# First stage of a two-block transformer kernel: x loaded first, squares summed on TensorE and VectorE, half of the modulation made as rows

## What is computed

```python
silu_c = jax.nn.silu(c)
silu_cc = jax.nn.silu(c_ctx)[None]
mod = jnp.split((silu_c @ ada_w[l] + ada_b[l])[:, None, :], N_MOD, axis=-1)
mod_c = jnp.split((silu_cc @ ada_w[l] + ada_b[l])[:, None, :], N_MOD, axis=-1)

def rmsnorm(x, g):
    xf = x.astype(jnp.float32)
    xf = xf * lax.rsqrt(jnp.mean(xf * xf, axis=-1, keepdims=True) + EPS)
    return (xf * g.astype(jnp.float32)).astype(x.dtype)

def modulate(h, shift, scale):
    return h * (1.0 + scale) + shift

t_ctx = mixer_inputs(modulate(rmsnorm(xc, norm_mix_g[l]), mod_c[0], mod_c[1]), w_in[l], ...)
t_lat = mixer_inputs(modulate(rmsnorm(x, norm_mix_g[l]), mod[0], mod[1]), w_in[l], ...)
```

## Time and profile before

| | us |
|---|---|
| median of 3 runs | 5051.04 |
| lowest and highest run | 5043.8 and 5053.86 |
| profiled execution | 5049.76 |
| its span, first to last instruction | 5047.7 |
| TensorE busy in it | 4843.0 (96%) |
| VectorE busy | 3071.4 (61%) |
| ScalarE busy | 1904.8 (38%) |
| GpSimd busy | 1260.1 (25%) |

### The profile page before, as it was taken

How to read it: one execution, slowest core, us unless ns; L and a number is a source line. 1 busy time by engine, 2 the same in 40 slices (tenths; PEclk the granted TensorE clock), 3 DMA queues, 4 the chain that set the end, 5 groups by cost and what they waited for, 6 DMA issues and landing times.

```text
span 5047.7 us, 66502 instructions
## 1 busy us (share of the span) xinstructions
PE 4843.0 (96%) x27141; PEld 4084.6 (81%) x27141; DVE 3071.4 (61%) x5232; ACT 1904.8 (38%) x2848; POOL 1260.1 (25%) x1007
## 2 busy tenths in 40 slices
PE   7999999999899999999999999999999899999999
PEld 6888878788779998987678787888888677767787
DVE  4545455689768898996543526366667444454555
ACT  3445322235833333333442426232223443353332
POOL 1111000036755666762220013100000210020000
PEclk8999999999999999999999999999999999999999
DMA  4111124423568998984101010222332121112222
GB/s 164 51 47 68 43 84 142 167 86 109 208 246 316 343 352 335 354 317 164 51 26 60 30 61 22 88 79 105 118 117 86 42 68 38 59 34 102 92 92 75
DMA packets 157310, 636.24 MB, mean 126 GB/s; under 512 B 12384, under 2 KB 62704, under 8 KB 106448
## 3 DMA queue, kind: packets, MB, share of 16 engines
q1 hardware_dynamic: 112688, 467.97, 25.5%
q0 software_dynamic: 42240, 160.88, 8.5%
q10 hardware_dynamic: 2080, 3.15, 0.2%
HBM read 595.25 MB, written 36.70 MB: 125 GB/s over the span
## 4 chain that ended last, share of the span: by engine, by line
PE 84%; DVE 7%; ACT 4%; POOL 2%; DMA 2%; issue 2%; SPq 0%; DVEq 0%; ACTq 0%; POOLq 0%
PE banks L280 70%; PE banks L3128 4%; PE banks L3247 2%; PE banks L3220 2%; DVE oa L2374 1%; PE banks L1020 1%; DMA X<-ctxT_in 1%; PE banks L396 1%; PE banks L358 1%; ACT high L214 1%; PE banks L952 1%; DVE nt L525 1%; PE banks L1011 1%; DVE cols L3152 1%; DVE low L229 1%
## 5 line engine op out<-in xcount | busy, mean ns | idle before, releaser
L229 DVE TENSOR_TENSOR low<-raw,high 128x2048 fp32r<-128x2048 f32 (+3 forms) x335 | 740.4, 2211 | 653.1 <-ACT high L214 653.0
L280 PE MATMUL banks<-UH,high 128*128 128x512 f32 (+2 forms) x2816 | 1041.7, 370 | 44.6 <-DVE UL L515 13.4
L280 PE MATMUL banks<-UH,low 128*128 128x512 f32 (+2 forms) x2816 | 1015.8, 361 | 0.0
L280 PE MATMUL banks<-UL,high 128*128 128x512 f32 (+2 forms) x2816 | 1015.4, 361 | 0.0
L214 ACT ACTIVATE high<-raw 128x2048 fp32r<-128x2048 f32 (+3 forms) x341 | 619.5, 1818 | 670.1 <-PE banks L280 332.4
L280 PEld LDWEIGHTS banks<-UH,high 128*128 128x128 f32 (+1 forms) x2816 | 533.1, 189 | 152.7 <-issue 51.8
L280 PEld LDWEIGHTS banks<-UH,low 128*128 128x128 f32 (+1 forms) x2816 | 533.5, 189 | 87.2
L280 PEld LDWEIGHTS banks<-UL,high 128*128 128x128 f32 (+1 forms) x2816 | 533.7, 190 | 79.9 <-issue 1.4
L280 PE MATMUL banks<-UpH,high 128*128 128x384 f32 (+1 forms) x1152 | 396.6, 344 | 3.8 <-ACT early L1995 2.9
L280 PE MATMUL banks<-UpL,high 128*128 128x384 f32 (+1 forms) x1152 | 395.5, 343 | 0.0
L280 PE MATMUL banks<-UpH,low 128*128 128x384 f32 (+1 forms) x1152 | 395.5, 343 | 0.0
(11 more groups left out here) (432 smaller groups left out, 9607.3 us busy)
## 6 DMA issues: line engine op xcount, KB each, us to landing
raw<-uT_in SPq DMA_DIRECT2D x64, 1024.0 KB, 6.1
raw<-ev_in SPq DMA_DIRECT2D x64, 1024.0 KB, 7.8
raw<-up_in SPq DMA_DIRECT2D x44, 1024.0 KB, 4.8
raw<-ada_in SPq DMA_DIRECT2D x40, 1024.0 KB, 4.9
side<-ada_in SPq DMA_DIRECT2D x24, 1024.0 KB, 9.9
raw<-gate_in SPq DMA_DIRECT2D x24, 1024.0 KB, 4.8
gt<-gd SPq DMA_DIRECT2D x31, 768.0 KB, 13.6
gd<-stage SPq DMA_DIRECT2D x11, 2048.0 KB, 6.4
```

The lines of the kernel that those rows point to most:

```text
L229: v.e.tensor_tensor(k.low[j % RAW][:, 0:w], k.raw[j % RAW][:, 0:w], k.high[i % SPL][:, 0:w].bitcast(F32), ALU.subtract).then_inc(*v.inc("w ...
L280: ins = pe.e.matmul(out, x, y, start=start and i == 0 and j == 0, stop=stop and i == n - 1 and j == 2)
```

## The change

X is loaded by SP, right behind `cf` and ahead of the modulation's tiles, instead of by ScalarE on its own queue. The modulation's tiles come in the order rows, cols, rows, cols, rows, cols, cols, rows.

The squares get eight buffers (the two, `sqsum` and five more), so that ScalarE makes all eight without a wait, after a table load that now comes ahead of the first. VectorE adds chunk 1 to 0, 4 to 3, and 6 and 7 to 5 (`ADDED`, four adds); TensorE sums the columns of 0, 2, 3 and 5 into the same bank (`first_sum_pe`, 24 products of one moving column). GpSimd adds nothing.

The scale is made as two rows: the two columns of `cf` are stationary, a tile's 256 columns are moving (`row` in `first_pe`, 32 products), the row goes by ScalarE to `crow` (`first_row_act`) and is turned to columns by TensorE (`turn`, eight transposes of 2x128). Rows, column sums, turns and the spread of the root are interleaved in the order that `first_pe` writes out.

The split of the third weight tile moves behind the normalisation on ScalarE and VectorE; the root's reciprocal moves between VectorE's dot products. The fourth copy of silu moves behind the squares on ScalarE. GpSimd stores `cs1` and `cs2` after the first two weight tiles have landed.

```diff
--- before.py
+++ after.py
@@ -612,44 +612,56 @@
     k.dots1 = Dots(k, "first", k.cs1)
     end, m.top = m.top, at
     k.n1 = NormMod(k, "n1", k.X, k.sc1, k.MOD[0][:, 0:8, :], k.U, BOTH, sums_at=end, sums=6, rows=2)
-    k.n1.s.added = "sq_sum_pool"
+    m.top = k.n1.s.end
+    k.n1.s.sq += [k.n1.s.acc] + [m.sb("sq", [128, T]) for _ in range(KC - 3)]
+    k.crow = m.sb("crow", [2, 256 * NFIRST])
     m.top = top
 
 
 def setup_sp(k):
     sp = k.sp
     sp.e.dma_start(k.cf[:], k.dram["cf"]).then_inc(*sp.inc("c_in", 0, by=16))
+    sp.e.dma_start(k.X[:, :, 0:TX], k.dram["xT"]).then_inc(*sp.inc("x_in", "x", by=16))
+    sp.e.dma_start(k.X[:, :, TX:T], k.dram["ctxT"]).then_inc(*sp.inc("x_in", "ctx", by=16))
     for t in range(NFIRST):
+        if t < NFIRST - 1:
+            first_rows_sp(k, t)
         sp.e.dma_start(k.first_cols[t][:], k.dram["adan"][t]).then_inc(*sp.inc(f"cols_in{t}", t, by=16))
-        sp.e.dma_start(k.first_rows[t][:], k.dram["ada"][t]).then_inc(*sp.inc(f"rows_in{t}", t, by=16))
+    first_rows_sp(k, NFIRST - 1)
     fill_raw(k, 2)
     for d in range(2):
         sp.e.dma_start(k.score[d][:], k.dram["causal"][d]).then_inc(*sp.inc("causal_in", d, by=16))
     fill_raw(k, RAW)
 
 
+def first_rows_sp(k, t):
+    sp = k.sp
+    sp.e.dma_start(k.first_rows[t][:], k.dram["ada"][t]).then_inc(*sp.inc(f"rows_in{t}", t, by=16))
+
+
 def setup_pool(k):
     g = k.pool
     g.e.dma_start(k.ident[:], k.dram["ident"]).then_inc(*g.inc("const_in", "ident", by=16))
     g.e.dma_start(k.vecs[:], k.dram["vecs"]).then_inc(*g.inc("vecs_in", 0, by=16))
-    for c in range(KC):
-        square_sum(g, k.n1.s, c)
 
 
 def setup_act(k):
     a = k.act
-    a.e.dma_start(k.X[:, :, 0:TX], k.dram["xT"]).then_inc(*a.inc("x_in", "x", by=16))
-    a.e.dma_start(k.X[:, :, TX:T], k.dram["ctxT"]).then_inc(*a.inc("x_in", "ctx", by=16))
     a.wait_ge("c_in", 0)
     a.e.activation(k.cft[:], k.cf[:], ACT.Exp, scale=-1.0).then_inc(*a.inc("setup_act", "c"))
     a.wait_ge("vecs_in", 0)
     for i in range(2):
         a.wait_ge("setup", ("lb", i))
         a.e.activation(k.lbt[1 + i][:], k.lbt[1 + i][:], ACT.Exp).then_inc(*a.inc("setup_act", ("lb", i)))
-    for i, cs in enumerate((k.cs1, k.cs2)):
-        for r in range(2):
-            a.wait_ge("mm", ("c", i, r))
-            a.e.activation(cs[:, r * D:(r + 1) * D], k.W[2 * i + r], ACT.Copy).then_inc(*a.inc("silu", ("c", i, r)))
+    silu_act(k, 0, 0)
+    silu_act(k, 0, 1)
+    silu_act(k, 1, 1)
+
+
+def silu_act(k, i, r):
+    a, cs = k.act, (k.cs1, k.cs2)[i]
+    a.wait_ge("mm", ("c", i, r))
+    a.e.activation(cs[:, r * D:(r + 1) * D], k.W[2 * i + r], ACT.Copy).then_inc(*a.inc("silu", ("c", i, r)))
 
 
 def setup_pe(k):
@@ -658,7 +670,7 @@
     for i in range(2):
         pe.wait_ge("setup", "c")
         pe.wait_ge("const_in", "ident")
-        for j in range(16):
+        for j in (range(16), (*range(8, 16), *range(8)))[i]:
             ins = pe.e.matmul(k.W[2 * i + j // 8][:, (j % 8) * 128:(j % 8 + 1) * 128], across(k.cf[:, 16 * i + j:16 * i + j + 1]), k.ident[:],
                               start=True, stop=True)
             if j % 8 == 7:
@@ -721,56 +733,123 @@
 def first_pe(k):
     pe = k.pe
     cf = k.cf[:].rearrange("p (i r c) -> p i r c", i=2, r=2)
-    for t in range(NFIRST):
+
+    def row(t):
         pe.wait_ge(f"cols_in{t}", t)
         pe.wait_ge("silu", ("c", 0, 0))
+        pe.wait_ge("silu", ("c", 0, 1))
+        if t >= 3:
+            pe.wait_ge("crow", t - 3)
         tile = view(k.first_cols[t][:], KC)
-        for i in range(2):
-            c = 2 * t + i
-            for kk in range(KC):
-                ins = pe.e.matmul(k.B[0][:, 2 * c:2 * c + 2], tile[:, kk, 128 * i:128 * i + 128], cf[:, 0, :, kk],
-                                  start=kk == 0, stop=kk == KC - 1)
-            ins.then_inc(*pe.inc("mm", ("first_cols", c)))
+        for kk in range(KC):
+            ins = pe.e.matmul(k.B[1 + t % 3][0:2, 0:256], cf[:, 0, :, kk], tile[:, kk, :], start=kk == 0, stop=kk == KC - 1)
+        ins.then_inc(*pe.inc("mm", ("first_row", t)))
+
+    def turn(t):
+        pe.wait_ge("crow", t)
+        for c in (2 * t, 2 * t + 1):
+            ins = pe.e.transpose(k.B[0][:, 2 * c:2 * c + 2], k.crow[0:2, c * 128:(c + 1) * 128], k.ident[0:2, 0:2])
+        ins.then_inc(*pe.inc("mm", ("first_cols", t)))
+    pe.wait_ge("silu", ("c", 1, 1))
+    first_sum_pe(k, 0)
+    first_sum_pe(k, 2)
+    row(0)
+    first_sum_pe(k, 3)
+    first_sum_pe(k, 5)
+    row(1)
+    row(2)
+    turn(0)
+    turn(1)
     pe.wait_ge("silu", ("c", 1, 0))
-    pe.wait_ge("silu", ("c", 1, 1))
-    norm_mod_pe(k, k.n1)
+    rows_pe(k, k.n1.s, 0)
+    row(3)
+    turn(2)
+    turn(3)
+    keep_clock(k, k.n1.s.sums, 4)
     pe.mark("first")
 
 
+ADDED = {0: (1,), 3: (4,), 5: (6, 7)}
+
+
+def first_sum_pe(k, c):
+    pe, s = k.pe, k.n1.s
+    if c in ADDED:
+        pe.wait_ge("sq_sum", (s.name, ADDED[c][-1]))
+    else:
+        pe.wait_ge("sq_act", (s.name, c))
+    for n in range(s.nt):
+        ins = pe.e.matmul(s.sums[:, n:n + 1], s.sq[c][:, n * 128:(n + 1) * 128], k.ones[:, 0:1], start=c == 0 and n == 0, stop=c == 5,
+                          skip_group_check=True)
+    if c == 5:
+        ins.then_inc(*pe.inc("mm", (s.name, "sum")))
+
+
+def first_add_dve(k, c):
+    v, s = k.dve, k.n1.s
+    v.wait_ge("sq_act", (s.name, c))
+    for d in ADDED[c]:
+        v.wait_ge("sq_act", (s.name, d))
+        if d - 1 in ADDED[c]:
+            v.wait_ge("sq_sum", (s.name, d - 1))
+        v.e.tensor_tensor(s.sq[c][:], s.sq[c][:], s.sq[d][:], ALU.add).then_inc(*v.inc("sq_sum", (s.name, d)))
+
+
+def first_row_act(k, t):
+    a = k.act
+    a.wait_ge("mm", ("first_row", t))
+    a.e.activation(k.crow[0:2, 256 * t:256 * t + 256], k.B[1 + t % 3][0:2, 0:256], ACT.Copy).then_inc(*a.inc("crow", t))
+
+
 def first_act(k):
-    a = k.act
+    a, s = k.act, k.n1.s
+    root_table(k, s)
     a.wait_ge("x_in", "x")
     a.wait_ge("x_in", "ctx")
     for c in range(KC):
-        square_act(k, k.n1.s, c, k.X[:, c, :])
-    root_act(k, k.n1.s)
+        a.e.activation(s.sq[c][:], k.X[:, c, :], ACT.Square).then_inc(*a.inc("sq_act", (s.name, c)))
+    silu_act(k, 1, 0)
+    first_row_act(k, 0)
+    root_act(k, s)
+    first_row_act(k, 1)
+    first_row_act(k, 2)
+    fill_hi(k, 2)
+    first_row_act(k, 3)
+    norm_mod_act(k, k.n1)
     fill_hi(k, ahead(k, 0))
-    norm_mod_act(k, k.n1)
     a.mark("first")
 
 
 def first_dve(k):
     v = k.dve
     v.wait_ge("silu", ("c", 0, 1))
+    first_add_dve(k, 0)
     for t in range(NFIRST):
         v.wait_ge(f"rows_in{t}", t)
         dots_dve(k, k.dots1, k.first_rows[t], t, t, k.MOD[0], ("tile", t))
+        if t == 0:
+            first_add_dve(k, 3)
+            first_add_dve(k, 5)
+        if t == 1:
+            root_dve(k, k.n1.s)
     bias_dve(k, k.MOD[0], vec(k, "ada_b"), 0, 8, ("first", 4 * NFIRST - 1), "first")
-    v.wait_ge("mm", ("first_cols", KC - 1))
+    fill_lo(k, 2)
+    v.wait_ge("mm", ("first_cols", NFIRST - 1))
     v.e.tensor_tensor(k.MOD[0][:, 8:16, :], k.B[0][:, 0:16].rearrange("p (c r) -> p c r", r=2), spread(vec(k, "ada_b")[:, 8:16], 2),
                       ALU.add).then_inc(*v.inc("ada_add", "scale"))
     v.wait_ge("ada_add", "scale")
     scale_dve(k, k.sc1, k.MOD[0][:, 8:16, :], vec(k, "norm_mix_g"), "b1")
-    root_dve(k, k.n1.s)
     v.wait_ge("scale", "b1")
+    norm_mod_dve(k, k.n1)
     fill_lo(k, ahead(k, 0))
-    norm_mod_dve(k, k.n1)
     v.mark("first")
 
 
 def first_pool(k):
 
     g = k.pool
+    for j in range(2):
+        g.wait_ge(f"w_raw{j}", j)
     for i, (name, cs) in enumerate((("cs", k.cs1), ("cs2", k.cs2))):
         g.wait_ge("silu", ("c", i, 0))
         g.wait_ge("silu", ("c", i, 1))
```

## The result

The changed kernel takes 5023.08 us (median of 4 runs, 5021.22 to 5023.74), the kernel before, run beside it, 5051.47 (4 runs, 5043.8 to 5053.86): a ratio of 0.9948 with a 95% interval of 0.9937 to 0.996, that is 20 to 32 us less. The forecast of 5027 is 4 us above it. The profiled execution after took 5023.74 us (span 5022.4), 26.0 less than the one before.

What follows compares the result with a forecast made beforehand. TensorE holds 84% of the span, but late X delays the start, then VectorE's chain sets "nt". Gains of 21.1 to 22.6 us, with 1.5 added, make 23: 5049.76 - 23 = 5026.8, rounded 5027; range 5018 to 5038.

Steps and rivals of the forecast that it cites:

- the middle of the two clocks: TensorE before "nt": clock lost while it waits and sums until about 25 us, regained halfway through row 0; gain 21.1.
- X first: X's load on SP's queue: begun at 2.1 us, landed at 11.3 to 14.3, before ScalarE can use it.
- up to 2 us sooner: Setup products, which waited for ident until 7.55 us, may start up to 2 us sooner; kept out of the times.
- 1.5 of 3.5 us: Ident's up to 2 us and the shorter pause before the projections, up to 1.5 us; only 1.5 of these counted.
- middle case: "nt" at about 47.5 us with TensorE's clock lost, then regained in row 0; VectorE waits 1.4 us for the root.
- loses seven sums of 1.80: GpSimd's term: it no longer makes seven sums of 1.80 us each.
- D: X late after all, landing at 42 us: "nt" at 70.6, 5052 us, 2 us slower; chance 3%.
- E: Nothing comes through: later stages shift against the clock's falls and the gain is lost, 5049 us; chance 2%.
- B: TensorE at half clock throughout: gain 4 to 6 us, 5044 to 5046; chance 10%.
- C: Clock late or falling between rows, or a weight tile after 42 us: gain 11 to 18, 5032 to 5039; chance 9%.
- F: More than forecast: all of the 3.5 us and no clock loss, gain 26 to 28, 5022 us; chance 4%.
- A: The forecast itself: 5022 to 5031 us; chance 72%.

Runs made afterwards that it cites:

- run without idle work: Changed kernel without the four unused TensorE products (keep_clock) behind the last turn: "nt" (first normalised rows) at 45.38 us, ratio to before 0.996.
- run with two-column products: Changed kernel with the scale made again by 64 products with two moving columns, in the rows' places, without turns: "nt" at 56.95 us, 5037.84 us, ratio 0.9979.
- warm sums: Changed kernel plus eight unused TensorE products in its pause ahead of the first column sums: "nt" at 43.81 us, copy of "gr" 69.37, ratio to before 0.9957.
- the second time: Changed kernel, unaltered, timed again: 5025.72 us (6 runs), "nt" at 45.56 us, ratio to before 0.9946.
- warm sums with longer idle work: Changed kernel with eight unused products ahead of the sums and nine instead of four behind the last turn: "nt" at 43.96 us, 5023.31 us, ratio 0.9955.
- X beside: Changed kernel with X's two loads back on ScalarE's queue beside the modulation's tiles: "nt" at 73.21 us, ratio to before 1.001.
- two adds: Changed kernel with four unused products ahead of the sums and two of VectorE's four adds given to TensorE as column sums: "nt" at 45.37 us, ratio 0.9956.
- GpSimd busy: Changed kernel plus seven GpSimd adds of 128x768 that nobody needs, from the end of VectorE's first add: "nt" at 51.90 us, one run.

## Why the prediction was right

The mechanism held: X was late because its queue shared the DMA engines with that of the tiles, VectorE's chain of dot products sets the end once X is early, and TensorE took the middle of the two clocks.

- *X first.* Forecast to land at 11.3 to 14.3 us; it landed 11.8 us after an issue at 1.88, at 13.7. It cost nothing: ScalarE came to it at 15.3. No row tile was waited for.
- *ScalarE.* The squares started at 15.31, not 17.35. The reason is the term that I kept out of the times, "up to 2 us sooner" for ident: it landed at 4.6 instead of 7.5, so the setup products began 2.9 us earlier. The run with X on ScalarE's queue again has them at 7.39, so it was X's place on that queue, beside the tiles, that held ident. The forecast counted 1.5 of 3.5 us for this and the clock at the projections together; they came to some 2 (squares) and 1.5 us. **This is the mis-sized term**: the whole 3.5 came. Without ident's 2 us the 23.5 at "nt" would be 21.5, inside the forecast's 21.1 to 22.6; with them and the 1.5 it is the 25.0 at the copy of "gr", against my 23.
- *VectorE.* First add 0.96 us (forecast 0.95), a row tile 4.8 us, three adds 2.88; every mark from 16.91 on lies 2 to 2.5 us before the forecast's middle case, which is ScalarE's 2 us above all. The wait for the root was 1.44 us; that case had 1.4. At the end VectorE's lows (44.69) and TensorE's last turn (44.58) came within 0.1 us of one another, where the case had TensorE last.
- *TensorE.* Sums 2.69 (2.71), row 0 5.45 (5.3), the other sums 2.84 (2.6), rows 1 and 2 7.07 (7.0), row 3 3.62 (3.5). The clock fell behind a wait and returned halfway through row 0, as assumed. That it did so just there was in part luck, as the run without idle work shows, but luck worth little: its "nt" is within 0.4 us of the change's. The run with two-column products shows the other answer was a real one: the same places cost 11.9 us more at 0.50.
- *TensorE's pauses.* The prediction took a shorter pause before the projections for a gain of up to 1.5 us, and the gain came: with a pause of 1.93 us they ran at 1.00, while the clock was 0.50 to 0.54 behind pauses of 3.85 us (no idle work) and 3.10 us (warm sums). The length of the pause is not all of it: in the run with X first alone a pause of 2.00 us was followed by 0.59 (56 to 60 us).
- *GpSimd.* Its stores were issued at 38.25, took 8.0 us and not 5.2, and nothing in the chain waits for them. But "loses seven sums of 1.80" was too small an account of it. Beside VectorE's dot products an add costs 2.3 to 2.7 us in three runs, and the dot products 2.4 to 2.8. The forecast needed no price for this, since the change has no such add; an account of what each part is worth did, and two of my expectations missed for want of it.
- *The rivals.* D (X late after all) did not come, but its mechanism did when X was put back: landing at 40.6 us, "nt" 73.21, later than the 70.6 that D had for a landing at 42. D had moved VectorE's chain (46.0) as it was, which for a landing at 40.6 gives 69.2; it left out that TensorE would end last, as in the middle case (47.5), and that, idle until the squares, it would start at a lower clock (0.59 from 43 to 57 us), with rows at 6.36 and 8.68 us. E did not come: the runs gained 20 to 32 us, and 20 to 35 the second time. B and C did not come, the clock being 1.00 from 28 us to the projections. Of F, the first half came, all of the 3.5 us, and the second did not, since the clock was lost until 26 us; the time alone, 5023, would not have told A from F.

What stays open: why the clock falls where it does behind waits and sums. Rows 1 and 2 took 7.07 us in four traces (the change twice, warm sums, warm sums with longer idle work) and 8.37 to 8.76 in four others with the same sums or more ahead of them (X beside, no idle work, two adds, GpSimd busy). The runs show that the fall moves, with the sums and without them, not what decides it.

## What to carry to other kernels

When a late transfer is brought forward, look at which engines' work comes to lie side by side that lay one behind the other before; here GpSimd's adds met VectorE's dot products and gave back part of the gain. Parts of a change can need one another: read each part's worth with the others in place, for alone one of these was a loss. And if an engine's chain is shortened by a microsecond, look at the pause that this opens further on: on TensorE it can cost the clock, and with it what was won, as with the warm sums.

## What the runs showed of the hardware that I had not expected

- A VectorE dot product (two operands in SBUF) of 1.22 us and a GpSimd add of 1.80 us, side by side, come in pairs of about 2.75 us (2.4 in the run with adds that nobody needs); three VectorE adds of 2.88 us in all take 6.48 beside GpSimd adds. Both engines show as busy all the time.
- TensorE can be busy without a pause from 20 to 56 us and be granted 0.50 throughout, with two moving columns per product; behind sums with one moving column the clock fell too (0.71 and 0.50 from 20 to 24 us in the run with warm sums, though it had been 1.00 from 16 to 20 us).
- Two traces of one order can differ in where the clock falls: behind the same wait of 3.49 us the first twelve sum records took 2.69 us in the change and 1.47 in the run without idle work.
- A small load on a third queue (ident, 64 KB) took 3.0 to 3.4 us in the ten traces with X behind `cf` on SP's queue and 6.0 and 6.2 in the two with X on ScalarE's, beside the tiles: where a large load stands changes what the small ones beside it take.
